# Splitting every weight slab on GpSimd by one whole copy and one whole subtraction

## The chip, the cores and the metric

One core of a Trainium2 chip runs the program. The metric is the device time of one execution in microseconds (us), and the time of the kernel before is the median of 3 runs.

## What is computed

The reference is two transformer blocks in a row over 512 tokens of width 1024. Cut to its steps:

```python
# first block
mod = silu(c) @ w_ada + b_ada                     # six vectors: shift, scale, gate, twice
h = modulate(rmsnorm(x, g_mix), sh1, sc1)
q, k, v, u_pool, b_gate, c_gate, x_conv = split(h @ w_in)
y_a = rmsnorm(diff_attention(q, k, v, lam, slopes), g_subln)   # two softmaxes, subtracted
y_b = multiscale_pool(u_pool, w_pool, pool_scale)              # windows 2, 4, 8, 16
y_c = short_gated_conv(b_gate, c_gate, x_conv, conv_w)         # three taps
x = x + gt1 * (concat(y_a, y_b, y_c) @ w_out)
x = x + gt2 * ((silu(h2 @ w_gate) * (h2 @ w_up)) @ w_down)     # h2 = modulated rmsnorm
x = rmsnorm(x, g_final)
# second block
z = rmsnorm(x, norm1_g) @ w_in_2                  # three attentions and their gates
x = x + (g0 * (fox @ w_fox_o) + g1 * (swa @ w_swa_o) + g2 * (mem @ w_mem_o)) @ w_out_2
# 8 heads pick 16 of 16384 experts each
a = h @ u[experts]; x = x + (gelu(a) * gates) @ v[experts]
```

Everything is float32.

## The kernel before

**Products.** A float32 product is made of three products of the rounded format fp32r: the operand is split into a high part (the value rounded to fp32r) and a low part (value minus high part), and hi x hi, hi x lo and lo x hi are summed in PSUM. So each weight and each activation exists as a pair, `W_hi`/`W_lo` and `A_hi`/`A_lo` or `B_hi`/`B_lo`.

**Weights.** All weights come as a stream of slabs, each 128 partitions x 2048 columns (1 MB). SyncE loads a slab into one of two places of `raw`; GpSimd splits it into one of two places of `W_hi` and `W_lo`; TensorE multiplies with it, in most stages 48 products of 512 columns. The 24 slabs of the modulation (`w_ada`) are not split: they are multiplied by `c` on VectorE or GpSimd and summed on ScalarE. After them `N_MID` = 93 slabs serve the two blocks up to the query projection of the experts, and 2 x `PAIRS` = 128 slabs hold the experts: 64 of `u`, the first 8 of which alternate with the query slabs, and 64 of `v`. The experts are computed densely: all of `u`, a gelu, a gate that is zero for the ones not picked, all of `v`.

**Splitting.** GpSimd takes the slabs in order. `split(s, j)` (lines 387 to 408) is used for slabs 0 to 93. It waits for the load (`slab_loaded`) and for TensorE having released the place two slabs before (`slab_used`), and then works in four quarters of 512 columns: high 0, high 1, low 0, high 2, low 1, high 3, low 2, low 3. The high part is `raw + zero` with a broadcast column of zeros (line 395), the low part is `raw - W_hi` (line 401), each low waiting on `slab_half` for its high. Only the last quarter's low raises `slab_split`. `split_whole` (lines 377 to 385) is used for slabs 94 to 220: the same two steps on all 2048 columns at once (lines 381 and 384). TensorE waits for `slab_split` of a slab before its first product with it, and SyncE waits for it before it loads the next slab into that place of `raw`. Between slabs 9 and 10 GpSimd multiplies 16 modulation slabs by `c` (line 421).

**Around it.** Stages are divided by `stage()` and `stage_end()`: TensorE, ScalarE and VectorE wait for one another there. VectorE instructions that the working below speaks of:
- Line 1449 (`gain`) and line 1458 make the first norm's gain from the modulation; `A_lo` comes from line 1303 behind it. `behind_split` on TensorE (lines 509 to 529, products at 521 to 523) starts with the first `A_lo` or `B_lo` and takes one more for each k step.
- Lines 1484 to 1505 compute the gated convolution, low parts (line 1275) and pooling sums; `diff_ready` (line 1506) releases the pooling product on TensorE (line 661). Nearly all their operands are in SBUF.
- Attention: per unit (a head and a block of 128 queries) TensorE makes scores (lines 590 and 593), VectorE adds the bias and takes the maximum (lines 1358 to 1376), ScalarE the exponential, VectorE normalises (line 1396 and 1397 in the differential one, line 1400 in the other three), TensorE transposes (line 602) and multiplies with the values (line 613). In the second block TensorE also makes gate projections between units (lines 631 to 633), for which one slab is released every one or two heads.
- `head_norm`: line 1270 (reciprocal) and line 1326 (scaling), once per tile.
- Merging of the branches swa and mem: eight times line 1598 (gate times PSUM) and line 1600 (sum of two SBUF tiles), one waiting for the other.
- Experts' `v`: line 1693 multiplies gelu and gates, ScalarE takes the high part (line 1223), line 1699 the low part; TensorE's products are lines 820 to 822. `u`: lines 754 to 756.

Of the kernel before, what the change touches and what calls it, by code (L numbers as in the profile page):

```python
# [6 lines left out]
P = 128  # L7
# [16 lines left out]


SLAB = 2048
PARTS = 4
PART = SLAB // PARTS
N_ADA = 6 * D // 256
ADA_FIRST = 8  # L30
ADA_LATER_AT = 10
N_MID = 93
IN_PARTS = N_MID + N_MID % 2
PAIRS = KEYS // 2
GT = 64
GB = T // GT
# [6 lines left out]
F32 = mybir.dt.float32  # L43
# [3 lines left out]
ALU = mybir.AluOpType  # L47
# [39 lines left out]
def build(nc, x_in, stream, cols_in, tables_in, mem_in, keys_in, out):  # L87
# [3 lines left out]
    with ExitStack() as ctx:  # L91
        def sb(name, shape, dt=F32):
            return ctx.enter_context(nc.sbuf_tensor(name, shape, dt))

        def sem(name):
            return ctx.enter_context(nc.semaphore(name))
# [11 lines left out]
        raw = sb("raw", [P, 2, SLAB])  # L108
        with nc.sbuf_tensor("W_plain", [P, 4, SLAB], F32) as W_plain:
            pass  # L110
        W_hi = sb("W_hi", [P, 2, SLAB], F32R)
        W_lo = sb("W_lo", [P, 2, SLAB], F32R)
# [5 lines left out]
        gs = sb("gs", [P, 2, KD])  # L118
        small = sb("small", [P, 48])
        zero = sb("zero", [P, 1])  # L120
        arena = sb("arena", [P, ARENA])
        bank = [ctx.enter_context(nc.psum_tensor(f"bank{i}", [P, 512], F32)) for i in range(8)]

# [69 lines left out]
        slab_loaded = [sem("slab_loaded0"), sem("slab_loaded1")]  # L193
# [4 lines left out]
        slab_half = sem("slab_half")  # L198
        slab_split = sem("slab_split")
        slab_used = sem("slab_used")  # L200
# [93 lines left out]
        def ada_rows(slab):  # L294

            return slab.rearrange("p (m i) -> p m i", m=2)
# [77 lines left out]

        @block.gpsimd
        def _(pool):
            def split_whole(s, j, ada=N_ADA - 4):

                pool.wait_ge(slab_loaded[j], s * 8 + (8 * ada + 16))
                pool.wait_ge(slab_used, s + (j - 1))  # L380
                pool.tensor_tensor(W_hi[:, j, :], raw[:, j, :], zero[:, :].to_broadcast([P, SLAB]), ALU.add)\  # L381
                    .then_inc(slab_half, 1)
                pool.wait_ge(slab_half, s + (IN_PARTS * (PARTS - 1) + j + 1))
                pool.tensor_tensor(W_lo[:, j, :], raw[:, j, :], W_hi[:, j, :].bitcast(F32), ALU.subtract)\  # L384
                    .then_inc(slab_split, 1)

            def split(s, j, ada=N_ADA - 4):

                pool.wait_ge(slab_loaded[j], s * 8 + (8 * ada + 16))
                if not isinstance(s, int) or s >= 2:  # L390
                    pool.wait_ge(slab_used, s + (j - 1))

                def high(part):
                    cols = slice(PART * part, PART * part + PART)
                    pool.tensor_tensor(W_hi[:, j, cols], raw[:, j, cols], zero[:, :].to_broadcast([P, PART]), ALU.add)\  # L395
                        .then_inc(slab_half, 1)

                def low(part):
                    cols = slice(PART * part, PART * part + PART)
                    pool.wait_ge(slab_half, s * PARTS + (PARTS * j + part + 1))  # L400
                    return pool.tensor_tensor(W_lo[:, j, cols], raw[:, j, cols], W_hi[:, j, cols].bitcast(F32),  # L401
                                              ALU.subtract)

                high(0)
                for part in range(1, PARTS):
                    high(part)
                    low(part - 1)
                low(PARTS - 1).then_inc(slab_split, 1)

            pool.memset(zero[:, :], 0.0).then_inc(zero_ready, 1)  # L410
            pool.wait_ge(zero_ready, 1)
            n = N_MID + 2 * PAIRS
            for s in range(0, ADA_LATER_AT, 2):
                for j in range(2):
                    split(s, j, ADA_FIRST - 4)
            pool.wait_ge(c_ready, 2)
            for s in range(ADA_FIRST, N_ADA):

                pool.wait_ge(slab_loaded[s % 2], 8 * (s - s % 2 + ADA_LATER_AT - 4) + 16)
                w = ada_rows(raw[:, s % 2, :])  # L420
                pool.tensor_tensor(w, w, c_rows, ALU.mult).then_inc(ada_times_c, 1)
            with pool.Fori(ADA_LATER_AT, IN_PARTS - 1, 2) as s:
                for j in range(2):
                    split(s, j)
            with pool.Fori(IN_PARTS, n - n % 2 - 1, 2) as s:
                for j in range(2):
                    split_whole(s, j)
            if n % 2:
                split_whole(n - 1, 0)


        @block.tensor
# [404 lines left out]
        def _(act):  # L837
# [45 lines left out]
            def squares(name, ready=None):  # L883

                src, n, _, _, _ = NORMS[name]

                step(act.activation(small[:, 40:41], small[:, 0:1], ACT.Sqrt))
                for k in range(KD):
                    if ready:
                        ready(k)  # L890
                    if k >= 4:
                        take(square_summed)
                    act.activation(S[k % 4][:, 0:n], src[:, k, :], ACT.Square).then_inc(norm_square, 1)
# [7 lines left out]
            def norm(name):  # L901
                src, n, _, shift, to = NORMS[name]
                w = at_["work"]
                at_["work"] += 1
                act.wait_ge(work_ready[w % 2], w // 2 + 1)
                act.activation(bank[4 + w % 2][:, 0:n], bank[4 + w % 2][:, 0:n], ACT.Sqrt, bias=small[:, 0:1])\
                    .then_inc(root_ready, 1)
                if to and shift:
                    for k in range(KD):
                        take(whole_ready)  # L910
                        act.activation(A_hi[:, k, :], bank[6 + k % 2][:, :], ACT.Identity, bias=shift(k))\
                            .then_inc(hi_ready, 1)
                elif to:
                    split(KD, lambda k: bank[6 + k % 2][:, 0:n], to, n=n)
# [929 lines left out]
```

## Time and profile before

| | |
|---|---|
| median of 3 runs | 3182.46 us (3180.27 to 3184.03) |
| the profiled execution | 3184.12 us, of which the span of the profile is 3182.3 us |
| TensorE products (PE) busy | 2940.2 us, 92% of the span |
| TensorE weight loads (PEld) | 2366.9 us, 74% |
| GpSimd (POOL) | 2061.2 us, 65% |
| VectorE (DVE) | 1763.3 us, 55% |
| ScalarE (ACT) | 659.3 us, 21% |
| DMA | 402 MB, 126 GB/s on average |
| granted TensorE clock, mean | 0.95 of full |

All times in the profile are in us from the span's start unless marked ns. A group of instructions is shown with its line, engine, operation, output and inputs, shape and count. A product of 512 columns is recorded with 390 ns although one starts every 0.23 us, since products overlap. In square brackets behind an instruction of the timeline stands how long its engine idled before it and what ended that.

### The profile page before, as it was taken

What the parts mean: (1) busy time and instruction counts of PE and PEld (TensorE: products, weight loads), DVE (VectorE), ACT (ScalarE), POOL (GpSimd) and SP (SyncE); (2) the same over time, 40 slices, a digit from 0 to 9 for tenths busy, and PEclk for the clock granted to TensorE, in tenths of its full rate; (3) what the DMA queues carried; (4) which work ended last, traced back from release to release, by engine and by line L of the source; (5) the groups of instructions that cost most, each with busy time, mean ns of one, the idle gap of its engine ahead of it and who ended that gap; (6) DMA issues with size and microseconds to landing.
All of it is one profiled execution on the core that took longest, in us unless ns stands there. A gap on an engine that the chain in (4) does not pass through costs nothing.

```text
span 3182.3 us, 39769 instructions
## 1 busy us (share of the span) xinstructions
PE 2940.2 (92%) x13562; PEld 2366.9 (74%) x13562; DVE 1763.3 (55%) x3055; ACT 659.3 (21%) x1262; POOL 2061.2 (65%) x1027
## 2 busy tenths in 40 slices
PE   4967699999899989899899999999999999999998
PEld 3754478888576655777787788888887788888886
DVE  4579831111355346634789755555555666666664
ACT  4145410001223324332101111111111101001000
POOL 3833468888552434858566766666666788888885
PEclk8966699999989989999999999999999999999999
DMA  5212212222210111222223344444445555555553
GB/s 223 93 60 86 100 66 93 93 105 94 71 67 27 40 57 40 100 73 80 94 102 117 139 159 172 172 172 172 172 172 188 182 185 198 197 185 196 199 185 132
DMA packets 126528, 402.19 MB, mean 126 GB/s; under 512 B 7504, under 2 KB 74704, under 8 KB 93904
## 3 DMA queue, kind: packets, MB, share of 16 engines
q1 hardware_dynamic: 113280, 328.75, 29.6%
q10 hardware_dynamic: 13136, 71.89, 5.7%
q8 instruction: 77, 1.26, 0.2%
q14 instruction: 35, 0.29, 0.0%
HBM read 331.40 MB, written 69.21 MB: 126 GB/s over the span
## 4 chain that ended last, share of the span: by engine, by line
PE 84%; DVE 8%; issue 3%; ACT 2%; POOL 2%; DMA 2%; ACTq 0%; SPq 0%; DVEq 0%; POOLq 0%
PE bank L820 7%; PE bank L822 7%; PE bank L821 7%; PE bank L487 7%; PE bank L489 7%; PE bank L488 7%; PE bank L754 7%; PE bank L756 7%; PE bank L755 7%; PE bank L805 4%; PE bank L613 2%; PE bank L631 2%; DVE arena L1396 2%; PE bank L602 1%; PE bank L633 1%
## 5 line engine op out<-in xcount | busy, mean ns | idle before, releaser
L395 POOL TENSOR_TENSOR W_hi<-raw,zero 128x512 fp32r<-128x512 f32 x376 | 404.4, 1086 | 526.9 <-PE bank L633 240.3
L381 POOL TENSOR_TENSOR W_hi<-raw,zero 128x2048 fp32r<-128x2048 f32 x127 | 457.4, 3602 | 430.4 <-PE bank L756 298.4
L384 POOL TENSOR_TENSOR W_lo<-raw,W_hi 128x2048 fp32r<-128x2048 f32 x127 | 639.5, 5036 | 9.9
L401 POOL TENSOR_TENSOR W_lo<-raw,W_hi 128x512 fp32r<-128x512 f32 x376 | 507.4, 1361 | 0.0
L754 PE MATMUL bank<-A_hi,W_hi 128*128 128x512 f32 x1024 | 446.5, 436 | 4.0 <-ACT B_plain L1164 2.9
L820 PE MATMUL bank<-B_hi,W_hi 128*128 128x512 f32 x1024 | 399.1, 390 | 10.4 <-DVE B_lo L1699 10.4
L755 PE MATMUL bank<-A_lo,W_hi 128*128 128x512 f32 x1024 | 401.3, 392 | 0.0
L756 PE MATMUL bank<-A_hi,W_lo 128*128 128x512 f32 x1024 | 401.1, 392 | 0.0
L821 PE MATMUL bank<-B_lo,W_hi 128*128 128x512 f32 x1024 | 398.8, 389 | 0.0
L822 PE MATMUL bank<-B_hi,W_lo 128*128 128x512 f32 x1024 | 398.8, 389 | 0.0
L1685 DVE TENSOR_SCALAR arena<-bank,arena 128x128 f32<-128x128 f32 x512 | 179.9, 351 | 293.6 <-PE bank L805 275.4
L1693 DVE TENSOR_TENSOR arena<-arena 128x1024 f32<-128x1024 f32 x64 | 231.2, 3613 | 139.1 <-DMA arena<-gates_dram 139.1
L1699 DVE TENSOR_TENSOR B_lo<-arena,B_hi 128x1024 fp32r<-128x1024 f32 x64 | 233.0, 3641 | 112.9 <-ACT B_hi L1223 112.9
L487 PE MATMUL bank<-A_hi,W_hi 128*128 128x512 f32 x680 | 266.0, 391 | 6.5 <-issue 2.8
L489 PE MATMUL bank<-A_hi,W_lo 128*128 128x512 f32 x680 | 264.7, 389 | 0.0
L488 PE MATMUL bank<-A_lo,W_hi 128*128 128x512 f32 x680 | 264.6, 389 | 0.0
L820 PEld LDWEIGHTS bank<-B_hi,W_hi 128*128 128x128 f32 x1024 | 192.6, 188 | 50.7 <-issue 10.7
L805 PEld LDWEIGHTS bank<-arena 128*128 128x128 f32 x1024 | 192.4, 188 | 43.1
L756 PEld LDWEIGHTS bank<-A_hi,W_lo 128*128 128x128 f32 x1024 | 192.7, 188 | 42.1
L821 PEld LDWEIGHTS bank<-B_lo,W_hi 128*128 128x128 f32 x1024 | 192.6, 188 | 40.0
L822 PEld LDWEIGHTS bank<-B_hi,W_lo 128*128 128x128 f32 x1024 | 192.5, 188 | 40.1
L754 PEld LDWEIGHTS bank<-A_hi,W_hi 128*128 128x128 f32 x1024 | 194.6, 190 | 24.2 <-issue 4.6
(232 smaller groups left out, 5000.5 us busy)
## 6 DMA issues: line engine op xcount, KB each, us to landing
raw<-weights SPq DMA_DIRECT2D x241, 1024.0 KB, 4.8
gelu_dram<-B_plain ACTq DMA_DIRECT2D x64, 512.0 KB, 2.7
gates_dram<-arena ACTq DMA_DIRECT2D x8, 4096.0 KB, 13.2
arena<-gelu_dram SPq DMA_DIRECT2D x64, 512.0 KB, 5.6
arena<-gates_dram SPq DMA_DIRECT2D x64, 512.0 KB, 6.8
W_plain<-weights SPq DMA_DIRECT2D x4, 1024.0 KB, 15.8
X<-x_t SPq DMA_DIRECT2D x1, 2048.0 KB, 14.2
out_t<-X SPq DMA_DIRECT2D x1, 2048.0 KB, 7.2
```

Source lines behind the costliest of these rows:

```text
L381: pool.tensor_tensor(W_hi[:, j, :], raw[:, j, :], zero[:, :].to_broadcast([P, SLAB]), ALU.add)\
L384: pool.tensor_tensor(W_lo[:, j, :], raw[:, j, :], W_hi[:, j, :].bitcast(F32), ALU.subtract)\
L401: return pool.tensor_tensor(W_lo[:, j, cols], raw[:, j, cols], W_hi[:, j, cols].bitcast(F32), ALU.subtract)
L487: mm(to, lh, rh, start=i == 0, stop=False)
L488: mm(to, lh, rl, start=False, stop=False)
L489: last = mm(to, ll, rh, start=False, stop=i == n - 1)
L754: mm(bank[6 + j][:, :], lh, rh, start=k == 0, stop=False)
L755: mm(bank[6 + j][:, :], lh, rl, start=False, stop=False)
L756: last = mm(bank[6 + j][:, :], ll, rh, start=False, stop=k == KD - 1)
L820: mm(bank[m][:, :], lh, rh, start=first and j == 0, stop=False, skip_group_check=True)
L821: mm(bank[m][:, :], lh, rl, start=False, stop=False, skip_group_check=True)
L822: last = mm(bank[m][:, :], ll, rh, start=False, stop=final and j == 1, skip_group_check=True)
```

## The change

`split_whole` goes, and with it the quarters. Every slab from 0 to 220 is split by one function, `split`, in two whole instructions. The high part is no longer an addition of zero but a `tensor_copy` from `raw` (float32) to `W_hi` (fp32r); in front of it GpSimd adds two single columns of zeros into a new tile `beat` of one column, which nothing reads. The waits on `slab_loaded` and `slab_used` are the same. The low part waits on `slab_half` for the copy and raises `slab_split`. The second loop over slabs is merged into the first.

```diff
         @block.gpsimd
         def _(pool):
-            def split_whole(s, j, ada=N_ADA - 4):
-
-                pool.wait_ge(slab_loaded[j], s * 8 + (8 * ada + 16))
-                pool.wait_ge(slab_used, s + (j - 1))
-                pool.tensor_tensor(W_hi[:, j, :], raw[:, j, :], zero[:, :].to_broadcast([P, SLAB]), ALU.add)\
-                    .then_inc(slab_half, 1)
-                pool.wait_ge(slab_half, s + (IN_PARTS * (PARTS - 1) + j + 1))
-                pool.tensor_tensor(W_lo[:, j, :], raw[:, j, :], W_hi[:, j, :].bitcast(F32), ALU.subtract)\
-                    .then_inc(slab_split, 1)
-
             def split(s, j, ada=N_ADA - 4):
 
                 pool.wait_ge(slab_loaded[j], s * 8 + (8 * ada + 16))
                 if not isinstance(s, int) or s >= 2:
                     pool.wait_ge(slab_used, s + (j - 1))
-
-                def high(part):
-                    cols = slice(PART * part, PART * part + PART)
-                    pool.tensor_tensor(W_hi[:, j, cols], raw[:, j, cols], zero[:, :].to_broadcast([P, PART]), ALU.add)\
-                        .then_inc(slab_half, 1)
-
-                def low(part):
-                    cols = slice(PART * part, PART * part + PART)
-                    pool.wait_ge(slab_half, s * PARTS + (PARTS * j + part + 1))
-                    return pool.tensor_tensor(W_lo[:, j, cols], raw[:, j, cols], W_hi[:, j, cols].bitcast(F32),
-                                              ALU.subtract)
-
-                high(0)
-                for part in range(1, PARTS):
-                    high(part)
-                    low(part - 1)
-                low(PARTS - 1).then_inc(slab_split, 1)
+                pool.tensor_tensor(beat[:, :], zero[:, :], zero[:, :], ALU.add)
+                pool.tensor_copy(W_hi[:, j, :], raw[:, j, :]).then_inc(slab_half, 1)
+                pool.wait_ge(slab_half, s + (j + 1))
+                pool.tensor_tensor(W_lo[:, j, :], raw[:, j, :], W_hi[:, j, :].bitcast(F32), ALU.subtract)\
+                    .then_inc(slab_split, 1)
...
-            with pool.Fori(ADA_LATER_AT, IN_PARTS - 1, 2) as s:
+            with pool.Fori(ADA_LATER_AT, n - n % 2 - 1, 2) as s:
                 for j in range(2):
                     split(s, j)
-            with pool.Fori(IN_PARTS, n - n % 2 - 1, 2) as s:
-                for j in range(2):
-                    split_whole(s, j)
             if n % 2:
-                split_whole(n - 1, 0)
+                split(n - 1, 0)
```

## Rows read from the trace of the kernel before

**Rows 1.** The page, busy us of each engine over the whole span.

```profile
PE 2940.2 (92%) x13562; PEld 2366.9 (74%) x13562; DVE 1763.3 (55%) x3055; ACT 659.3 (21%) x1262; POOL 2061.2 (65%) x1027
```

**Rows 2.** Stretches: length, busy PE, PEld, DVE, ACT, POOL, clock, DMA, GB/s.

```profile
1760.00:2480.00 720.00, 707.03 (x3613) 600.07 (x3612) 394.39 (x1047) 137.50 (x241) 443.91 (x108) 0.99 0.47 172
2480.00:3182.00 702.00, 689.76 (x3044) 570.80 (x3042) 457.13 (x131) 65.75 (x62) 562.39 (x124) 0.99 0.53 182
```

**Rows 3.** TensorE's waits from 371 us: total us, times, longest.

```profile
PE bank L820 <- DVE B_lo L1699: 10.4, 1, 10.4
PE bank L487 <- POOL W_lo L401: 8.5, 6, 3.1
```

**Rows 4.** GpSimd's groups by shape: count, busy us, mean ns, idle before.

```profile
L384 POOL TENSOR_TENSOR W_lo<-raw,W_hi 128x2048 fp32r<-128x2048 f32 x127 | 639.5, 5036 | 9.9
L401 POOL TENSOR_TENSOR W_lo<-raw,W_hi 128x512 fp32r<-128x512 f32 x376 | 507.4, 1361 | 0.0
...
L395 POOL TENSOR_TENSOR W_hi<-raw,zero 128x512 fp32r<-128x512 f32 x376 | 404.4, 1086 | 526.9 <-PE bank L633 240.3 <-PE bank L523 109.5 <-PE bank L489 108.3
```

**Rows 5.** Timeline in the tail: start, duration, instruction, [idle before it].

```profile
2694.80 5.46 POOL L384 TENSOR_TENSOR W_lo<-raw,W_hi 128x2048 fp32r<-128x2048 f32 x1
2702.07 3.60 POOL L381 TENSOR_TENSOR W_hi<-raw,zero 128x2048 fp32r<-128x2048 f32 x1 [1.80 <-PE bank L822]
...
2697.63 3.72 DVE L1693 TENSOR_TENSOR arena<-arena 128x1024 f32<-128x1024 f32 x1 [1.82 <-DMA arena<-gates_dram]
2703.05 3.70 DVE L1699 TENSOR_TENSOR B_lo<-arena,B_hi 128x1024 fp32r<-128x1024 f32 x1 [1.70 <-ACT B_hi L1223]
```

**Rows 6.** Timeline at the start, TensorE and VectorE.

```profile
51.23 0.80 PE L521 MATMUL bank<-A_hi,W_hi 128*128 128x512 f32 x1 [21.62 <-POOL W_lo L401]
...
44.35 1.18 DVE L1449 SCALAR_TENSOR_TENSOR gs<-mod,col 128x8 f32<-128x8 f32 x1
```

**Rows 7.** Timeline of the pooling sums and the product behind them.

```profile
127.25 1.43 DVE L1498 TENSOR_TENSOR arena<-arena 128x525 f32<-128x525 f32 x1
...
147.66 2.83 PE L661 MATMUL bank<-arena,col 64*64 64x512 f32 x6 [4.93 <-DVEq L1506]
```

**Rows 8.** Timeline in swa attention, one split and VectorE's scaling.

```profile
1185.94 0.35 DVE L1400 TENSOR_SCALAR arena<-arena,small 128x256 f32<-128x256 f32 x1
1198.40 1.14 DVE L1400 TENSOR_SCALAR arena<-arena,small 128x256 f32<-128x256 f32 x1
...
1196.12 2.04 POOL L395 TENSOR_TENSOR W_hi<-raw,zero 128x512 fp32r<-128x512 f32 x2 [39.01 <-PE bank L633]
...
1199.60 0.44 PE L602 MATMUL bank<-tab,arena 128*128 128x128 f32 x2 [0.27 <-DVE arena L1400]
```

**Rows 9.** Timeline in fox attention, one split and the transposes behind it.

```profile
1020.11 2.04 POOL L395 TENSOR_TENSOR W_hi<-raw,zero 128x512 fp32r<-128x512 f32 x2 [22.39 <-PE bank L633]
...
1025.84 0.55 PE L602 MATMUL bank<-tab,arena 128*128 128x128 f32 x3
```

**Rows 10.** Timeline of the swa branch's merging, and TensorE's next stage.

```profile
1282.44 2.49 POOL L395 TENSOR_TENSOR W_hi<-raw,zero 128x512 fp32r<-128x512 f32 x2 [3.17 <-PE bank L523]
...
1294.03 0.69 DVE L1600 TENSOR_TENSOR arena<-arena 128x512 f32<-128x512 f32 x1
...
1294.87 0.47 PE L487 MATMUL bank<-A_hi,W_hi 128*128 128x512 f32 x1 [1.70 <-DVEq L1246]
```

**Rows 11.** Timeline: swa head norm, and TensorE's first product after swa attention.

```profile
1151.18 1.36 DVE L1326 SCALAR_TENSOR_TENSOR arena<-arena,small 128x512 f32<-128x512 f32 x1
...
1271.17 0.47 PE L521 MATMUL bank<-B_hi,W_hi 128*128 128x512 f32 x1 [2.81 <-DVE B_lo L1275]
```

**Rows 12.** Timeline after the mem merging: TensorE's first product, slab freed.

```profile
1461.14 0.77 PE L521 MATMUL bank<-B_hi,W_hi 128*128 128x512 f32 x1 [4.14 <-DVE B_lo L1275]
...
1473.96 2.04 POOL L395 TENSOR_TENSOR W_hi<-raw,zero 128x512 fp32r<-128x512 f32 x2 [3.84 <-PE bank L523]
```

More of the change, by code:

```diff
@@ L26 @@
 SLAB = 2048
-PARTS = 4
-PART = SLAB // PARTS
 N_ADA = 6 * D // 256
@@ L32 @@
 N_MID = 93
-IN_PARTS = N_MID + N_MID % 2
 PAIRS = KEYS // 2
@@ L120, in build @@
         zero = sb("zero", [P, 1])
+        beat = sb("beat", [P, 1])
         arena = sb("arena", [P, ARENA])
```

## The prediction

> **What bounds the kernel now.** I read the busy line first: TensorE 92%, GpSimd 65%, VectorE 55% [rows 1]. The stretches say where the rest is: from 1760 us to the end TensorE is busy for 1397 of 1422 us [rows 2], so the streams of expert slabs are bound by TensorE (64 slabs in 702 us, 10.9 us and a little for each), and GpSimd's splitting is hidden there: before its W_hi of 2702.07 it idles 1.80 us until TensorE frees the place [rows 5]. What the change can move lies in the first 1540 us, where TensorE idles at stage borders and in attention. The list of TensorE's waits after 371 us [rows 3] names GpSimd for only 8.5 us in 6 waits; VectorE is named more often (L820, L521, L602 in rows 3, 11 and 8). So the question is what the split does to VectorE.
>
> **How the two engines meet.** L1693 starts at 2697.63, while a W_lo that began at 2694.80 runs until 2700.26; it ends at 2701.35, 1.1 us after that. L1699 starts at 2703.05 behind the W_hi of 2702.07 to 2705.67 and ends at 2706.75, again 1.1 us later [rows 5]. Both have two SBUF inputs. So such an instruction waits until the GpSimd instruction in front is over, however long it is; the GpSimd instruction behind it then loses about 0.45 us (5.46 against the mean of 5.04 in rows 4). L1400, a scaling with one SBUF input, does the same: 0.35 us alone, 1.14 us inside a split [rows 8]. Instructions with an input in PSUM, as L1598, pass. In the parted split a GpSimd instruction lasts 1.0 to 1.4 us [rows 4, 8] and VectorE gets in after each: 1.43 us apiece in the chain before 147 us [rows 7], where a free one takes 0.69 [rows 10]. A whole W_lo bars VectorE for 5.0 us at one go.
>
> The rule behind this is in the Trainium skill, SBUF — State Buffer, "Who interferes with whom": the pair of ports that both engines use is locked for a whole instruction and not shared by bandwidth. It speaks against this change, and the trace agrees. If the pair were shared instead, the second rival would hold.
>
> **The new split's price.** For each of the first 94 slabs (376 quarters) it takes out 4 x 1.086 + 4 x 1.361 = 9.8 us, contention included, and puts in a one-column add, a copy and a W_lo of 5.04 us [rows 4]. No row shows a copy on GpSimd. Between 512 columns (1.02 us, half of the 2.04 pair in rows 8) and 2048 (3.60) the present W_hi costs 1.68 ns a column and 0.17 us fixed, and it reads two streams. The copy reads one; at half of that per column it is 0.17 + 1.72 = 1.9 us, with the small add (0.17 fixed) 2.1 us. Ends: 1.8 us (half of 3.60) and 5.04 (as dear as the subtraction). I take 2.1: W_lo against W_hi shows that time follows the streams read. A slab is then 7.1 us. The third rival has the upper side.
>
> The Trainium skill, GPSIMD Engine Reference, "Engine selection", calls one-input work roughly line-rate on GpSimd; with the 128 lanes and 1.2 GHz that it lists this would be an estimate of 1.7 us. No run here shows it yet.
>
> TensorE is released by slab_split at the very end of a slab both before and after, so no finer hand-over is lost; behind GpSimd's new wait on slab_half only its own W_lo is queued. SyncE's next load starts up to 2 us sooner, and no wait for a load is on TensorE's path there.
>
> Below, t0 is when a slab's place is free; W_hi then takes to t0 + 2.1 and W_lo to t0 + 7.1 (7.5 if VectorE gets in between). Each term is a delay of TensorE:
>
> 1. Start and conv/pool chain, **+3.4**. TensorE's first product waits for the first split (51.23). This would be 2 us sooner, but L1449 (44.35) [rows 6], on which A_lo hangs, lands behind the whole W_lo (44.3 to 49.3), and A_lo comes at 51.6: +0.4. Then L1484 to L1505, all on SBUF: of a slab's 10.9 us GpSimd bars 7.1 to 7.9 and lets two through; in the 3 us left VectorE does four: six, where 1.5 us apiece is seven. The last 17, stepped one by one from 120.4 us, end at 151.0 and not 147.6; once TensorE stalls, GpSimd runs dry and VectorE is free. L661 waits for the last one already (4.93 us) [rows 7], so it all counts, and about 2 us of waits for GpSimd that go before it only lengthen that wait.
> 2. Fox attention, three splits, **+5**. t0 = 1020.11: L1400 is ready at 1023.1, inside W_lo, and ends at 1027.5; the transposes L602 take its result at 1025.84 [rows 9]: 1.7 us each.
> 3. Swa attention, three splits, **+11**. t0 = 1196.12: L1400 is ready at about 1198.5 and ends at 1203.3; L602 takes it at 1199.60 and waits 0.27 already [rows 8]: 3.6 us each. TensorE is otherwise full here, so nothing is caught up. In mem attention L602 comes late enough: 0.
> 4. Merging of the swa branch, **+8**. t0 = 1282.44. Eight pairs of L1598 (free) and L1600 (two SBUF inputs): the second L1600 waits for the copy (1285.2), the third for W_lo (1290.6); when TensorE frees the next place at about 1293, the sixth waits for the copy (1296.2), the seventh for W_lo (1301.6). The eighth ends at 1303.0 and not 1294.7, and TensorE stands at this stage's end already (1.70 us) [rows 10].
> 5. Merging of the mem branch, **+7.5**: the same pattern; 0.8 comes back, since L1275 behind it, for which TensorE waits 4.14 us [rows 12], runs free.
> 6. Head norms and first operands, **+7**. L1326 at 1151.18 takes 1.36 us [rows 11]; it would wait for W_lo until 1155.2 (+2.7), and the next one, now barred, is free (-1.1): +1.6. The same stepping gives +1.0 behind diff attention, +1.3 in mem, and 0 in fox, which has slack. After swa attention (place free 2.81 us before 1271.17) [rows 11] the first L1275 still gets in behind the copy; the second waits for W_lo to t0 + 8.1, while TensorE is through its twelve products of 0.23 us at t0 + 5.6: +2.5. After fox and mem it restarts slowly: +0.3 each.
> 7. Gains, **-3.6**. In the last gate/up group the w_down slabs have only 36 products (8.2 us), and TensorE waits for GpSimd: -2 of the 8.5. The tail's first B_lo comes behind a copy and not a 3.6 us add: its 10.4 us wait [rows 3] loses 1.6. The mem projections' part of the 8.5 goes too, but there the head norms then set the end (in 6).
> 8. Clock, **+2**. After a pause of 4.14 us the first product takes 0.77 us (the granted clock at half, 1.2 GHz) and the slab 12.8 us (1461.14 to 1473.96) [rows 12]; after 2.81 us it was 0.47 us and 11.3 (1271.17 to 1282.44) [rows 10, 11]. The new pause of 10 us before 1303 costs about 1.5 to 1.9. The swa stalls might add up to 1.5 each; that is in the range.
>
> The gate/up groups cost nothing: L1275 may be barred for 5 us, but has 10.9; behind a group's last slab TensorE has seven k steps (9.5 us) before it takes the last B_lo. From 1760 us on nothing but the 1.6 changes, as long as copy and small add stay under 3.6 + 1.8 = 5.4 us.
>
> Sum: 3.4 + 5 + 11 + 8 + 7.5 + 7 - 3.6 + 2 = **+40 us** on the profiled execution of 3184.1 (its span 3182.3 and 1.8 around it), which is 1.6 over the median of 3182.5. On the median: 3223.
>
> **Rivals.**
> A. Stalls absorbed: attention's queues have more slack than one split shows; chain and merges alone decide (3.4 + 8 + 7.5 - 3.6): 3198. For it: L1400's 1.14 us now costs TensorE 0.27. Against: the time at which L602 takes the result is in the rows.
> B. Faster, by sharing: VectorE suffers by the share of time that GpSimd reads, not by the length of one instruction. A slab falls from 9.8 to 7.1 us; the waits for GpSimd go (8.5 and 2), 2 at the start, 1.6 at the tail, and a quarter of the chain's 14 us of delay: about -17, 3166. It decides if a barred L1600 is back in under 2.5 us. Against: L1693 in rows 5.
> C. The copy is no quicker than the add (3.6): W_hi ends 1.5 us later at some 14 places, the chain takes 3 more: +25 more, 3248. For it: there is no row of a copy.
> D. The copy is over 5.4 us: GpSimd then bounds both streams, each us above costs over 125, and 6 us of copy give 3330 with the terms above. Only the conversion speaks for it.
> E. No effect: the new delays fall into idle time and so do the gains: 3182.
>
> **Chances.** Forecast 0.56, A 0.13, B 0.10, C 0.14, D 0.03, E 0.04. The range leaves out at most 0.2 (B, D, E and a little): from 3194, a little under A, to 3254, C with the clock's stalls. A change of 0.2% (6 us) can be told from none: faster 0.10 (B), same 0.05, slower 0.85.
>
> **What would show it.** Afterwards: a GpSimd copy of about 1.9 us; L1400 of 4 to 5 us at the swa splits and L602 waiting some 3.6 us for it three times; L1600s of about 2.5 and 5 us, and TensorE waiting some 10 us at the stage's end behind them, twice; L661 waiting about 10 us; a tail that keeps its 10.9 us. It would be wrong if W_lo yields to VectorE midway, if VectorE loses or wins the race at t0 + 2.1 otherwise than stepped (one race decides 5 us), or if the copy is not near 2 us.

## The result, and the profile after

| | before | after |
|---|---|---|
| median | 3183.24 us (3180.27 to 3185.1, 4 runs) | 3218.42 us (3210.8 to 3221.2, 4 runs) |
| ratio after/before | | 1.0108, 95% interval 1.0089 to 1.0127 |
| profiled execution, and its span | 3184.12, 3182.3 us | 3210.80, 3209.0 us |

The change makes the kernel 35 us slower; the forecast was 3223 (3194 to 3254). The profiled execution of after is the quickest of its four, so its trace accounts for 26.7 us of the 35; a second profile (first experiment) is of a slower one.

In the kernel after, lines behind the split stand 27 lower than in the kernel before: L575 is the old L602, L1373 the old L1400, L1573 the old L1600, L494 the old L521, L460 the old L487, L634 the old L661, L1248 the old L1275, L1672 the old L1699. GpSimd's three instructions are L380 (`beat`), L381 (the copy) and L383 (W_lo).

The page of after: busy time of the engines, and two GpSimd groups (count, busy us, mean ns, idle before).

```profile
PE 2952.2 (92%) x13562; PEld 2373.0 (74%) x13562; DVE 1716.7 (53%) x3055; ACT 659.3 (21%) x1262; POOL 1606.9 (50%) x684
...
L383 POOL TENSOR_TENSOR W_lo<-raw,W_hi 128x2048 fp32r<-128x2048 f32 x221 | 1080.7, 4890 | 17.7
...
L381 POOL CAST W_hi<-raw 128x2048 fp32r<-128x2048 f32 x221 | 421.1, 1905 | 0.0
```

GpSimd has 454 us less to do than in [rows 1], and the copy takes the 1.9 us that the prediction took. None of it reaches the end, because TensorE's waits grew. TensorE's waits from 371 us in the kernel after (total us, times, longest):

```profile
PE bank L494 <- DVE B_lo L1248: 28.0, 8, 9.4
PE bank L566 <- ACTq L822: 22.7, 2, 13.8
PE bank L575 <- DVE arena L1373: 20.8, 11, 3.6
...
PE bank L460 <- issue: 10.6, 4, 7.8
...
PE bank L793 <- DVE B_lo L1672: 4.4, 1, 4.4
```

TensorE no longer waits for W_lo (8.5 us in [rows 3]), but it waits for VectorE 20.8 us in attention, where it was 9.1, and 7.8 us behind the swa merging ("issue": no releaser is recorded), where it was 1.70 [rows 10].

**Swa attention**, timeline of one split in the kernel after (start, duration, instruction, [idle before]); it answers to [rows 8].

```profile
1193.45 1.90 POOL L381 CAST W_hi<-raw 128x2048 fp32r<-128x2048 f32 x1
...
1195.43 4.50 POOL L383 TENSOR_TENSOR W_lo<-raw,W_hi 128x2048 fp32r<-128x2048 f32 x1
1195.59 4.49 DVE L1373 TENSOR_SCALAR arena<-arena,small 128x256 f32<-128x256 f32 x1
...
1200.14 0.69 PE L575 MATMUL bank<-tab,arena 128*128 128x128 f32 x2 [3.60 <-DVE arena L1373]
```

The scaling, 0.35 us alone [rows 8], starts 0.16 us into W_lo and ends 0.15 us behind it; TensorE stands for 3.60 us. The two other splits of this stage cost 3.54 and 3.60 us. What follows a stall is in the stretches behind it (length, busy PE, PEld, DVE, ACT, POOL, granted clock, DMA share, GB/s):

```profile
1190.00:1196.50 6.50, 6.50 (x28) 3.92 (x27) 4.17 (x12) 3.12 (x10) 3.10 (x3) 1.00 0.00 0
1200.10:1204.00 3.90, 3.86 (x11) 2.83 (x12) 1.69 (x7) 1.06 (x4) 0.00 (x0) 0.50 0.76 252
1204.00:1208.00 4.00, 4.00 (x11) 2.01 (x11) 1.57 (x6) 1.17 (x4) 0.00 (x0) 0.50 0.04 16
1208.00:1212.00 4.00, 4.00 (x16) 2.57 (x15) 1.22 (x5) 0.76 (x2) 0.00 (x0) 0.82 0.00 0
1212.00:1216.00 4.00, 4.00 (x18) 2.33 (x16) 2.41 (x9) 2.37 (x9) 0.00 (x0) 1.00 0.00 0
```

TensorE went into this stall at full clock (2.4 GHz) and came out at half (1.2 GHz); it does 11 products in 4 us, where it does 18 afterwards. Behind the second stall (to 1232.09) the granted clock is 0.66 in the first 3.9 us, behind the third (to 1261.55) 0.50 for 8 us again. In the shorter fox stall (1.05 us, to 989.42) the clock stays at 1.00 behind.

**Merging of swa**, timeline of the kernel after; it answers to [rows 10].

```profile
1303.33 4.94 POOL L383 TENSOR_TENSOR W_lo<-raw,W_hi 128x2048 fp32r<-128x2048 f32 x1
...
1304.55 4.26 DVE L1573 TENSOR_TENSOR arena<-arena 128x512 f32<-128x512 f32 x1
...
1313.67 4.82 POOL L383 TENSOR_TENSOR W_lo<-raw,W_hi 128x2048 fp32r<-128x2048 f32 x1
...
1314.17 0.69 DVE L1571 TENSOR_TENSOR arena<-B_lo_plain,bank 128x512 f32<-128x512 f32 x1
1314.89 4.15 DVE L1573 TENSOR_TENSOR arena<-arena 128x512 f32<-128x512 f32 x1
1319.19 0.76 PE L460 MATMUL bank<-A_hi,W_hi 128*128 128x512 f32 x1 [7.78 <-issue]
```

L1571, with one input in PSUM, takes 0.69 us inside W_lo; L1573, with both in SBUF, ends 0.54 us after W_lo has ended (1308.81 against 1308.27, 1319.04 against 1318.49).

### The profile page after: what moved, and what is told of

The parts are those of the page before. It is cut to its first block, busy times and chain, and to the rows that moved or that the text cites. A ratio compares the mean times of both kernels' runs of the same rounds, so it can differ in the third digit from the quotient of the medians.

```text
span 3209.0 us, 39173 instructions
## 1 busy us (share of the span) xinstructions
PE 2952.2 (92%) x13562; PEld 2373.0 (74%) x13562; DVE 1716.7 (53%) x3055; ACT 659.3 (21%) x1262; POOL 1606.9 (50%) x684
## 3 DMA queue, kind: packets, MB, share of 16 engines
q8 instruction: 77, 1.26, 0.2%
## 4 chain that ended last, share of the span: by engine, by line
PE 83%; DVE 11%; ACT 2%; issue 2%; DMA 1%; ACTq 0%; POOL 0%; SPq 0%; DVEq 0%; POOLq 0%
PE bank L460 7%; PE bank L793 7%; PE bank L794 7%; PE bank L795 7%; PE bank L461 7%; PE bank L462 7%; PE bank L727 7%; PE bank L729 7%; PE bank L728 7%; PE bank L778 4%; PE bank L586 2%; PE bank L604 2%; DVE arena L1243 2%; DVE arena L1369 2%; PE bank L575 1%
## 5 line engine op out<-in xcount | busy, mean ns | idle before, releaser
L383 POOL TENSOR_TENSOR W_lo<-raw,W_hi 128x2048 fp32r<-128x2048 f32 x221 | 1080.7, 4890 | 17.7
L380 POOL TENSOR_TENSOR beat<-zero 128x1 f32<-128x1 f32 x221 | 45.9, 208 | 1423.1 <-PE bank L729 421.2
L381 POOL CAST W_hi<-raw 128x2048 fp32r<-128x2048 f32 x221 | 421.1, 1905 | 0.0
L1666 DVE TENSOR_TENSOR arena<-arena 128x1024 f32<-128x1024 f32 x64 | 247.3, 3865 | 123.7 <-DMA arena<-gates_dram 123.7
L460 PE MATMUL bank<-A_hi,W_hi 128*128 128x512 f32 x680 | 266.4, 392 | 10.6 <-issue 10.6
L1672 DVE TENSOR_TENSOR B_lo<-arena,B_hi 128x1024 fp32r<-128x1024 f32 x64 | 132.5, 2071 | 206.6 <-ACT B_hi L1196 206.6
L728 PEld LDWEIGHTS bank<-A_lo,W_hi 128*128 128x128 f32 x1024 | 195.2, 191 | 19.5
```

Source lines behind the costliest of these rows:

```text
L381: pool.tensor_copy(W_hi[:, j, :], raw[:, j, :]).then_inc(slab_half, 1)
L460: mm(to, lh, rh, start=i == 0, stop=False)
L728: mm(bank[6 + j][:, :], lh, rl, start=False, stop=False)
```

## Experiments

Ratios are to the kernel before on the same chip (3182.7 to 3183.7 us in every comparison).

### The kernel after once more

> The changed kernel once more, for a second profile. Its four times so far are 3210.8 (the profiled one), 3218.3, 3218.6 and 3221.2 us. If the spread comes from races between VectorE and GpSimd, another execution should differ at single places by whole instructions of 2 or 4.6 us, the first at L1422 (0.17 us in the profile, where it slipped in ahead of W_lo; 4.7 us if it loses). If it comes from something else (clock, DMA), the places where VectorE waits are the same and the time differs evenly.

3215.65 us (3212.13 to 3225.99, 4 runs), ratio 1.0099 (1.0082 to 1.0116). Its profile is of the slowest execution (3225.99). The stalls are the same to 0.01 us (fox 1.05, 1.12, 1.05; swa 3.61, 3.54, 3.60). The other 15 us sit elsewhere, the largest parts being 3.7 by 396 us, most of it in diff attention, where TensorE's waits for the normalising come to 57.0 us and not 53.3; 2.0 in fox attention, where the clock is 0.96 in place of 0.99; 1.6 behind swa attention, where the second low part keeps TensorE waiting for 1.89 us and not 0.30; 4.35 in the tail, whose first product waits 8.77 us in place of 4.42. L1422 slipped in again. So only the tail differs by a whole instruction, as a race would have it; the rest is smaller steps and the clock. Against the profiled execution of before the cost is 27 us in the one and 42 in the other.

### Two whole instructions, the high part by an add

```diff
-                pool.tensor_tensor(beat[:, :], zero[:, :], zero[:, :], ALU.add)
-                pool.tensor_copy(W_hi[:, j, :], raw[:, j, :]).then_inc(slab_half, 1)
+                pool.tensor_tensor(W_hi[:, j, :], raw[:, j, :], zero[:, :].to_broadcast([P, SLAB]), ALU.add)\
+                    .then_inc(slab_half, 1)
```

> The change without its copy: every slab in two whole instructions, but the high part by the old addition of zero (3.6 us). Theory 1 (what costs is how long one GpSimd instruction bars VectorE): W_hi ends 1.6 us later wherever VectorE is barred, so slower than the changed kernel by 15 to 30 us: 3235 to 3250; L602 in swa attention (there L575) waits about 5.2 us instead of 3.6. Rival 2 (the converting copy is what hurts, the whole subtraction not): near the kernel before or faster, 3165 to 3185.

3259.75 us (4 runs), ratio 1.0242 (1.0225 to 1.0259): theory 1 has the sign and the swa stalls, but not the size, 44 us above the changed kernel where 15 to 30 were expected. W_hi now bars VectorE for 3.6 us, where the copy does for 1.9; each swa stall is 5.1 to 5.2 us, each fox stall 2.6 (1.05 to 1.12 with the copy), and the pooling product waits 14.5 us (8.9 with the copy). The cost of whole instructions by themselves is thus 77 us, and the copy gives 44 of it back (3259.75 against 3215.65 on the same chip): it isn't the copy that makes the changed kernel slow.

### W_lo in quarters again, the copy kept

```diff
-                pool.tensor_tensor(W_lo[:, j, :], raw[:, j, :], W_hi[:, j, :].bitcast(F32), ALU.subtract)\
-                    .then_inc(slab_split, 1)
+                for part in range(4 if parts else 1):
+                    w = SLAB // 4 if parts else SLAB
+                    cols = slice(w * part, w * part + w)
+                    last = pool.tensor_tensor(W_lo[:, j, cols], raw[:, j, cols], W_hi[:, j, cols].bitcast(F32), ALU.subtract)
+                last.then_inc(slab_split, 1)
```

`parts` is true for slabs 0 to 93 and false behind them.

> The changed kernel with its whole copy, but with the subtraction in four quarters for slabs 0 to 93; the rest as in the changed kernel. Theory 1: the longest bar is now the copy (1.9 us) and then 1.2 to 1.3 us, so nearly all of the +27 to +35 us goes: 3165 to 3180, a little under the kernel before, as a slab takes 7.3 us and not 9.2. Rival 2 (the copy hurts): 3205 to 3220. Rival 3 (what hurts is that GpSimd's work is one block, four reads in a row without a gap): little changes, over 3200.

3166.05 us (3163.66 to 3168.88, 4 runs), ratio 0.9948 (0.9932 to 0.9965): one edit turns 1% slower into 0.5% faster. Timeline of a swa split (lines are 21 below those of before; L1379 is the scaling, L581 the transposes):

```profile
1188.37 1.12 DVE L1379 TENSOR_SCALAR arena<-arena,small 128x256 f32<-128x256 f32 x1
1189.55 0.44 PE L581 MATMUL bank<-tab,arena 128*128 128x128 f32 x2 [0.71 <-DVE arena L1379]
```

The stall is 0.71 us and the transposes run at full clock (0.44 us, where they took 0.69). There are none in fox attention.

### Quarters and order as before, only the high part by copy

```diff
-                    pool.tensor_tensor(W_hi[:, j, cols], raw[:, j, cols], zero[:, :].to_broadcast([P, PART]), ALU.add)\
-                        .then_inc(slab_half, 1)
+                    pool.tensor_copy(W_hi[:, j, cols], raw[:, j, cols]).then_inc(slab_half, 1)
```

Slabs 94 to 220 get the whole copy of the changed kernel, and each slab has one `beat` ahead of it.

> The kernel before with its quarters and their order kept, and the high part by the converting copy everywhere (quarters for slabs 0 to 93, whole for the rest), one small add of one column ahead of each slab. Theory 1: bars of 0.6 and 1.3 us, a slab of about 7.5 us: faster than the kernel before by 10 to 20 us, 3163 to 3173. Rival 2 (the copy hurts): not faster than before, 3183 or more. If a copy has a large fixed cost, the quarters of it are dearer than 0.65 us each and the gain shrinks to under 5 us.

3173.43 us (7 runs), ratio 0.997 (0.9958 to 0.9981), at the upper edge of what was expected. A quarter of copy takes 0.68 us, four of them 2.7, where the whole takes 1.9. The two profiled executions are 9.5 us apart, and it lies in two places: swa attention lasts 112.9 us here against 108.1 (stalls of 1.26 us against 0.71), and the tail's first product waits 8.77 us against 4.39. So the bars are no longer than with one copy, yet the stalls are: the scaling waits out a quarter of W_lo in both (1.12 us), but reaches it later here, since the steps ahead of it had waited too (L1392, 0.92 us against 0.36).

### Whole W_lo in the three swa splits alone

```diff
+            with pool.Fori(64, 66, 2) as s:
+                split(s, 0)
+                split(s, 1, parts=False)
+            with pool.Fori(66, 68, 2) as s:
+                for j in range(2):
+                    split(s, j, parts=False)
```

This stands in the middle of the loop of the kernel with quarters: slabs 65, 66 and 67 are whole.

> The kernel with the low part in quarters (3166 us), but with W_lo whole again for the three slabs that are split during swa attention (slabs 65, 66 and 67), and for no other of the first 94. It prices term 3 alone, which stood at 11 us and came out as 16.4 in the stretch of the changed kernel. Theory T (a barred scaling stalls TensorE, and the stall takes the clock down as well): three stalls of about 3.6 us in place of 0.7, and the granted clock of swa attention falls from 0.98 to about 0.86, so that the stage grows by 14 to 17 us: 3180 to 3184. Theory U (the stalls alone; the low clock of the changed kernel came from somewhere else, such as the norm ahead of the stage): three times 2.9 us, 8.7 in all, with a clock of 0.95 or more: 3174 to 3176.

3183.52 us (10 runs), ratio 1.0003 (0.9994 to 1.0013), 17.5 us above the kernel with quarters. TensorE's first product of swa attention and the first one behind it, here and in the kernel with quarters:

```profile
1150.05 2.48 PE L581 MATMUL bank<-arena 64*128 64x128 f32 x6 [11.74 <-ACTq L837]
...
1218.58 0.69 PE L590 MATMUL bank<-tab,arena 128*128 128x128 f32 x2 [3.55 <-DVE arena L1388]
...
1273.67 0.47 PE L509 MATMUL bank<-B_hi,W_hi 128*128 128x512 f32 x1 [2.79 <-DVE B_lo L1263]
```

```profile
1150.54 2.48 PE L572 MATMUL bank<-arena 64*128 64x128 f32 x6 [11.74 <-ACTq L828]
...
1258.68 0.47 PE L500 MATMUL bank<-B_hi,W_hi 128*128 128x512 f32 x1 [2.79 <-DVE B_lo L1254]
```

The stage lasts 123.6 us and not 108.1: 15.5 us for three instructions kept whole. Of these, 8.7 are the stalls (3.61 + 3.55 + 3.61 against 0.71 + 0.70 + 0.70), and 6.8 are left for the clock, which is 0.88 of full here and 0.96 there. Theory T holds.

### W_lo in halves

As with quarters, with `range(2 if parts else 1)`.

> The changed kernel with W_lo in two halves of 1024 columns for slabs 0 to 93 (about 2.5 us each, where the whole lasts 4.9 and a quarter 1.2). Theory T (the cost is the length of one instruction, less the slack that TensorE has): the scaling in swa attention is barred 2.4 us less, so TensorE waits about 1.2 us there instead of 3.6, and not at all in fox attention; the waits behind the two mergings fall from 7.8 and 9.4 to about 4.5 and 6, the one for the pooling sums from 8.9 to about 6.5; with shorter stalls the clock stays up in swa attention (0.95 or more). About 30 of the 51 us between whole (3217) and quarters (3166) come back: 3180 to 3194. Theory V (what costs is that one instruction of GpSimd spans more than a VectorE step, however long): halves are like the whole, 3205 or more.

3181.44 us (10 runs), ratio 0.9993 (0.9984 to 1.0003). Timeline of a swa split:

```profile
1189.19 4.71 POOL L386 TENSOR_TENSOR W_lo<-raw,W_hi 128x1024 fp32r<-128x1024 f32 x2
1189.36 2.34 DVE L1379 TENSOR_SCALAR arena<-arena,small 128x256 f32<-128x256 f32 x1
1191.75 0.44 PE L581 MATMUL bank<-tab,arena 128*128 128x128 f32 x2 [1.46 <-DVE arena L1379]
```

The same scaling, starting at the same point of the split, is held 2.34 us by half a W_lo and 4.49 by a whole one, and the time and the stalls of 1.4 us are about what theory T says. The clock is not: the first transposes behind a stall still run at full clock (0.44 us), but then it falls. The stage and the 4 us behind each of its three stalls:

```profile
1155.50:1269.28 113.78, 104.55 (x424) 65.11 (x425) 67.25 (x202) 46.69 (x149) 22.86 (x15) 0.91 0.08 28
1191.75:1195.75 4.00, 4.00 (x13) 2.56 (x13) 3.82 (x7) 1.01 (x4) 2.16 (x1) 0.60 0.11 23
1218.90:1223.00 4.10, 4.09 (x13) 2.72 (x14) 3.82 (x7) 1.07 (x4) 2.17 (x1) 0.62 0.15 28
1246.20:1250.20 4.00, 3.99 (x13) 2.62 (x14) 3.83 (x7) 1.00 (x4) 2.17 (x1) 0.62 0.22 33
```

The stage is 5.6 us longer than with quarters; 2.2 of it are the stalls, and 3.4 are left for the clock (0.91 here, 0.95 or more expected). The waits behind the mergings are 3.3 and 6.1 (expected 4.5 and 6). The pooling product misses: 8.51 us (6.5 expected), hardly less than the 8.90 with whole ones, while quarters gave 4.85. The trace shows where: each of the last two sums of the chain waits out a half (2.71 us apiece, to 148.4), while with quarters the last takes 1.64 us and ends at 144.4.

### The merging's product and sum through PSUM

```diff
-                        tile(lambda b: dve.tensor_tensor(S[2], gate_t[i], b[:, :], ALU.mult))
+                        tile(lambda b: dve.tensor_tensor(bank[6][:, :], gate_t[i], b[:, :], ALU.mult))
...
-                        step(dve.tensor_tensor(merged[:, i, :], merged[:, i, :], S[2], ALU.add))
+                        step(dve.tensor_tensor(merged[:, i, :], merged[:, i, :], bank[6][:, :], ALU.add))
```

> The changed kernel, but in the merging of branches swa and mem the product of gate and branch is written to a free PSUM bank and added from there, so that the sum has one input in SBUF and one in PSUM. Everything on GpSimd is as in the changed kernel. Theory T (only an instruction with two inputs in SBUF, or a scaling with both sides there, is barred): the sums take about 0.7 us even inside a W_lo, the eight pairs end some 8 us sooner, and TensorE waits 1 to 2 us behind the swa merging (7.8 now) and 4 to 5 behind the mem merging (9.4 now): 3203 to 3208. Theory W (the sums are barred by their output or by their one SBUF input as well): the sums keep their mean of 1.8 us and the time stays at 3212 to 3220.

3207.02 us (3203.11 to 3210.91, 4 runs), ratio 1.0071 (1.0051 to 1.009). VectorE's sums of the swa merging, first in the kernel after, then here (mean ns):

```profile
L1573 DVE TENSOR_TENSOR arena<-arena 128x512 f32<-128x512 f32 x8 | 14.4, 1800 | 0.3
```

```profile
L1573 DVE TENSOR_TENSOR arena<-arena,bank 128x512 f32<-128x512 f32 x8 | 5.5, 686 | 0.3
...
1316.13 0.47 PE L460 MATMUL bank<-A_hi,W_hi 128*128 128x512 f32 x1 [1.70 <-issue]
```

One operand moved, GpSimd untouched, and not one sum is held: 1800 ns become 686, and TensorE's wait falls from 7.78 to the 1.70 us of before. This separates the cause from everything else that a W_lo does at that time. The whole time alone would not show it, since the interval overlaps that of the changed kernel (1.0082 to 1.0116). Behind the mem merging the wait falls only to 7.39 us (expected 4 to 5): the sums end early, and L1248, the first low part behind them with two inputs in SBUF, is now the one that meets W_lo.

### Quarters and PSUM together

> The kernel with W_lo in quarters (3166 us) with the same PSUM bank in both mergings. In quarters the merging's sums are barred 1.2 us at most, and TensorE waits 2.8 and 4.5 us behind the two mergings. Theory T: these waits fall to 1 to 1.5 and 3.5 to 4: 3163 to 3165, one to three us faster than with quarters alone. Rival: something behind the merging (the first low part, the load of weights) sets the end of the stage, and the time stays at 3166.

3161.68 us (3160.28 to 3165.29, 4 runs), ratio 0.9935 (0.9919 to 0.9952); the waits behind the mergings are 1.70 and 4.15 us (2.80 and 4.46 with quarters alone). The median is 4 us lower and the waits 1.4, and the two intervals overlap (0.9932 to 0.9965 with quarters alone), so the gain is read from the waits. This is, with the last one below, the fastest kernel of the study.

### The copy in the streams alone

```diff
             def split_whole(s, j, ada=N_ADA - 4):
...
-                pool.tensor_tensor(W_hi[:, j, :], raw[:, j, :], zero[:, :].to_broadcast([P, SLAB]), ALU.add)\
-                    .then_inc(slab_half, 1)
+                pool.tensor_tensor(beat[:, :], zero[:, :], zero[:, :], ALU.add)
+                pool.tensor_copy(W_hi[:, j, :], raw[:, j, :]).then_inc(slab_half, 1)
```

> The kernel before with one part of the change alone: slabs 94 to 220 get their high part by the whole copy (with the one-column add ahead of it) in place of the whole add of 3.6 us; slabs 0 to 93 keep their quarters and their adds. It prices the gain at the start of the last stream, which stood at 1.6 us in term 7. Theory T (behind the first gelu and gates, VectorE's multiplication and low part each wait for the GpSimd instruction in front; with a copy of 1.9 us they meet the copy and W_lo in either of two orders): TensorE's wait there is 4.4 or 8.8 us where it was 10.4, and nothing else moves: 3176 to 3181, with a stream of 10.9 us a slab as before. Rival G (the wait was set by the load of gelu and gates): no change, 3183.

3184.93 us (11 runs), ratio 1.0007 (0.9998 to 1.0016): theory T is wrong in the time, and rival G, whose time this is within the noise, in the reason. The wait did shrink, from the 10.4 us of [rows 3] to 4.33:

```profile
2466.32 1.23 DVE L1694 TENSOR_TENSOR arena<-arena 128x1024 f32<-128x1024 f32 x1 [24.75 <-DMA arena<-gates_dram]
2466.41 2.89 POOL L383 CAST W_hi<-raw 128x2048 fp32r<-128x2048 f32 x1
...
2468.67 1.71 DVE L1700 TENSOR_TENSOR B_lo<-arena,B_hi 128x1024 fp32r<-128x1024 f32 x1 [1.12 <-ACT B_hi L1224]
...
2470.52 0.77 PE L821 MATMUL bank<-B_hi,W_hi 128*128 128x512 f32 x1 [4.33 <-DVE B_lo L1700]
```

VectorE's product slips in 0.09 us ahead of the copy, and the low part meets the copy and not W_lo. But 1.5 us come back at the clock: behind the shorter wait TensorE is at half speed for over 4 us (0.50 in 2470.5 to 2474.7, where before has 0.65 in its first 4.2 us), so that the stretch from this product to the end lasts 712.0 us and not 710.5. Another 1.7 us had gone by the start of the experts' u stream, which is no more than single stages of two profiles of the kernel before differ by. And the u stream itself lost 3 us, with TensorE busy throughout. That asked for two more runs.

### The kernel before once more, and with the one-column add alone

```diff
+                pool.tensor_tensor(beat[:, :], zero[:, :], zero[:, :], ALU.add)
                 pool.tensor_tensor(W_hi[:, j, :], raw[:, j, :], zero[:, :].to_broadcast([P, SLAB]), ALU.add)\
                     .then_inc(slab_half, 1)
```

> The kernel before, unchanged, profiled on the chip of this comparison. In every other kernel the slabs of the experts' u stream with gate work between them go at 14.66 us where the kernel before shows 14.55, with TensorE busy without a gap in both, some 3 us over the stream; and the whole-add kernel has it too, whose GpSimd instructions there are the same as in the kernel before. Theory L (the pace comes with the program: TensorE's own steps are a little longer in any program that was edited): 14.55 again here. Rival M (it differs from chip to chip or from session to session): 14.66 here.

> The kernel before with nothing but the one-column add put ahead of the whole add of slabs 94 to 220. GpSimd's extra 0.2 us a slab lies in its idle time. Theory L: the u stream goes at 14.66 us a slab, since the program was edited, and the time is 3184 to 3187. Rival K (only the copy, or the shorter high part, changes that pace): 14.55, and the time stays at 3183.

3183.21 us (ratio 0.9998, 0.9989 to 1.0008) and 3185.93 us (ratio 1.001, 1.0001 to 1.0019). GpSimd's high parts in the u stream, first of the unchanged kernel, where TensorE releases each, then with the small add, which stands between:

```profile
2009.26 3.60 POOL L381 TENSOR_TENSOR W_hi<-raw,zero 128x2048 fp32r<-128x2048 f32 x1 [6.27 <-PE bank L756]
...
2023.94 3.60 POOL L381 TENSOR_TENSOR W_hi<-raw,zero 128x2048 fp32r<-128x2048 f32 x1 [6.39 <-PE bank L756]
...
2038.49 3.60 POOL L381 TENSOR_TENSOR W_hi<-raw,zero 128x2048 fp32r<-128x2048 f32 x1 [6.27 <-PE bank L756]
```

```profile
2009.81 3.60 POOL L383 TENSOR_TENSOR W_hi<-raw,zero 128x2048 fp32r<-128x2048 f32 x1
...
2024.60 3.60 POOL L383 TENSOR_TENSOR W_hi<-raw,zero 128x2048 fp32r<-128x2048 f32 x1
...
2039.25 3.60 POOL L383 TENSOR_TENSOR W_hi<-raw,zero 128x2048 fp32r<-128x2048 f32 x1
```

The steps are 14.68 and 14.55 us in the one, 14.79 and 14.65 in the other. TensorE has no idle time in 2010 to 2240 in either, at clock 1.00, yet does 1192 products there in the one and 1185 in the other. The slower pace is in every edited kernel, also in the whole-add one, whose GpSimd instructions in this stream are those of before. So rivals M and K fall, and some 3 us of the 35 come with the edit of the program and not with the copy or the length of the split. That any edit does it, as theory L says, is not shown: all the edited kernels, the whole-add one too, also have the new tile `beat`, which is allocated ahead of `arena`. In the u stream TensorE reads its gate work from `arena`, and only the slabs with gate work are slower (14.45 to 14.68 us before, 14.55 to 14.79 edited); those without take 10.8 to 11.2 us in both. Whether the place of the tiles or that of TensorE's instructions does it no run separates, and it stays open.

The two profiles of the unchanged kernel also say how well a stage's length is known: swa attention lasts 109.3 us in the one and 107.0 in the other, fox attention 141.2 and 143.2. TensorE's waits for the scaling in swa attention are 3.6 us in both; it is the granted clock that differs (0.93 and 0.95 in swa, 0.96 and 0.94 in fox).

### Quarters in the streams too

> The fastest kernel so far (copy whole, W_lo in quarters for slabs 0 to 93, the mergings' sums with an input in PSUM, 3161.7 us) with W_lo in quarters for slabs 94 to 220 too. Theory T (an SBUF instruction of VectorE waits for the GpSimd instruction in front): the first low part of the last stream is barred at most 1.9 us, TensorE's wait there is 4 us or less, never 8.8, and the streams, in which TensorE has 10.9 us for a slab and GpSimd now needs 7.5, keep their pace: 3159 to 3162, and less spread. Rival H (four instructions a slab cost GpSimd enough to hold TensorE in the streams, or their writes get in the way of the loads): 3170 or more.

3162.16 us (3160.11 to 3166.64, 5 runs), ratio 0.9937 (0.9924 to 0.9951): the same as with whole ones in the streams, and the spread is not less (6.5 us against 5.0). The tail's wait stays 4.39 us (4 or less was expected), since the low part there meets the copy, which is still whole. The streams keep their pace with four subtractions a slab; neither gain nor loss, as TensorE bounds them.

## Why the prediction was right, point by point

The time, the sign and the mechanism hold: an instruction of VectorE with two inputs in SBUF, or a scaling from SBUF to SBUF, lasts until the GpSimd instruction in front ends, and the price is that instruction's length less TensorE's slack. Three lengths of W_lo (4.9, 2.4, 1.2 us) gave swa stalls of 3.6, 1.4 and 0.7 us and 3218, 3181 and 3166 us; moving one operand to PSUM took the swa merging's loss away, and part of the mem merging's. These runs agree with the lock rule that the prediction weighed, in the Trainium skill, SBUF — State Buffer, "Who interferes with whom". Rival A falls with the stalls of 3.6 us, B with the halves (a share of time would not depend on the cut), C and D with the copy's 1.905 us, E with the time. The copy's price of 1.9 us was right, but the reason for taking it, that time follows the streams read, doesn't carry: W_hi and W_lo read two each and last 3.60 and 5.04 us. By lengths of stages in the two profiled executions, which for attention are good to some 2 us:

- **Term 1** (+3.4): -0.7; it failed in both halves. At the start L1422 (the old L1449) was ready 0.02 us before W_lo began (44.86 against 44.88) and got through in 0.17 us; the first product came at 49.46, 1.8 earlier and not 0.4 later. A_lo's instructions, with one input in PSUM, pass inside W_lo. From the first product to the pooling product it takes 97.6 us against 96.4, so +1.1 where +3.0 was stepped, and both halves together come to -0.7. The wait did grow, to 8.90 us (some 10 were named), but it begins earlier.
- **Term 2** (+5): +3.4. Each stall is 1.05 to 1.12 us and not 1.7, because an uncontended W_lo lasts 4.53 us there and I took 5.04, its mean in the streams; L1373 is let go half a microsecond sooner.
- **Term 3** (+11): the stalls are as said (3.6 three times), the stage is +16.4. The step that failed is term 8: the clock's share of "up to 1.5 each" was left in the range, and it is some 7 us for the three (6.8 in the kernel with these splits alone). This is the largest single error.
- **Term 4 with term 6's +2.5 and the clock's +2** (together +12.5): +8.3. The second low part after swa attention waited 0.30 us and not 2.5, since TensorE was still at its first twelve products, at a clock of 0.65 (in the other profile, at full clock, it waited 1.89); this slab took 13.4 us at clock 0.87; and W_lo caught the fourth and the eighth sum, not the third and the seventh, as the eight pairs had started by then.
- **Term 5** (+7.5): +5.8, the same pattern with the eighth sum held.
- **Term 6, norms**: swa +1.9 (fox's restart in it; predicted 1.6 + 0.3). Diff attention with its norms -1.6 and not +1.0 (+1.2 in the other profile of this kernel). Mem's norms +0.3 and not +1.3; mem attention, at 0 in the prediction, gained 2.2, and why stays open.
- **Term 7** (-3.6): the last FFN groups gave 3.3 and not 2. The tail's wait fell by 5.9 us and not 1.6 (VectorE's product got in just ahead of the copy; in the other profile it didn't, and the wait fell by 1.6), of which the clock took 1.5 back: from the tail's first product to the end it is 712.0 us and not 710.5. Against it stands what no step had: 3 us of slower pace in the u stream.

These stages add up to the +27 of the profiled execution, the quickest, where +40 was summed; the median is at +35 and the slower profile at +42. So the sum was near the +35 for partly wrong reasons: too much at the start, in fox and in the mergings, too little for the clock and nothing for the u stream. That these errors offset each other is luck; the range covered them.

## What to carry to other kernels

When one engine bars another for the length of an instruction, cut the barring instruction to the slack of whoever waits behind, and leave whole only what is short: here one copy of 1.9 us and four subtractions of 1.2 us beat both the uncut and the evenly cut split, although their engine is idle half the time. Or take the barred instruction out of reach by putting one operand in PSUM. And count the clock with each stall of a busy TensorE: three stalls that were 2.9 us longer apiece, 8.7 in all, cost 15.5, and three that were 0.7 longer, 2.2 in all, cost 5.6.

## What was not expected

- A stall of 3.6 us inside a stage that is otherwise full halves the granted clock for up to 8 us behind it (0.50 from 1200.1 to 1208.0). Stalls of 1.4 us do it too, for some 3 us (0.60 to 0.62 over 4 us behind each of the three with halves), and of the three of 1.26 us with quarters of copy one did (0.68, then 0.50) and two did not (1.00). Behind stalls of 1.05 to 1.12 us in fox and of 0.7 us with quarters it was 1.00.
- A copy with conversion on GpSimd is near half the price of an add with a broadcast column (1905 against 3602 ns for 128x2048) and costs 678 ns for 128x512, so cutting it in four adds 0.8 us.
- Which of VectorE and GpSimd goes first can hang on under 0.1 us (44.86 against 44.88 at the start, 2466.32 against 2466.41 in the tail); the race in the tail is worth 4.35 us (waits of 8.77 and 4.42 in two profiles of the same kernel). Eight executions of the kernel after spread over 15 us, four of the one with quarters over 5; but 18 of the kernel before on one chip over 11, so that the long instructions widen the spread is not shown.
- An edit that adds only one small GpSimd instruction and its tile of one column lengthened TensorE's gapless steps in one stream by 0.7% (14.55 to 14.65 us a slab), 3 us in all.
